# Feed-forward input products: the order of two loops in TensorE's stream

## The reference

```
def swiglu(h, w_in, w_out):
    gate, up = jnp.split(h @ w_in, 2, axis=-1)
    return (jax.nn.silu(gate) * up) @ w_out

x = x + 0.5 * swiglu(rmsnorm(x, norm_ffn1[layer]), w_ffn1_in[layer], w_ffn1_out[layer])
# mixer: retention in layer 0, sparse attention (indexer, top-k, latents) in layer 1
x = x + 0.5 * swiglu(rmsnorm(x, norm_ffn2[layer]), w_ffn2_in[layer], w_ffn2_out[layer])
```

## Time and profile before

| | |
|---|---|
| median of 3 runs | 1981.36 us (1980.68 to 1982.73) |
| profiled execution | 1981.29 us |
| its span, first to last instruction | 1979.5 us |
| mean granted TensorE clock in it | 0.997 |
| TensorE busy | 1952.8 us, 99% |
| VectorE busy | 1446.8 us, 73% |
| ScalarE busy | 887.1 us, 45% |
| low parts of group products (VectorE L1544) | 280, 1217 ns each |
| high parts of group products (ScalarE L1019) | 280, 1063 ns each |

### The profile page before, as it was taken

One profiled execution on the slowest core, in us unless ns is written; L12 is line 12 of the kernel. 1 busy time (PEld: TensorE's weight loads), 2 busy tenths in 40 slices (PEclk: granted clock), 3 DMA queues, 4 the chain that ended last, 5 costly groups with the idle time before them and its releaser, 6 DMA issues.

```text
span 1979.5 us, 23580 instructions
## 1 busy us (share of the span) xinstructions
PE 1952.8 (99%) x9152; PEld 1611.3 (81%) x9152; DVE 1446.8 (73%) x1838; ACT 887.1 (45%) x1240; POOL 219.3 (11%) x163
## 2 busy tenths in 40 slices
PE   8999999999999999999999999999999999999998
PEld 7788888878787878888888888888897888888886
DVE  7999953876666859999943899984358769989732
ACT  5545632342424435545621555562168445554510
POOL 0000011100000022000021000002145440000121
PEclk9999999999999999999999999999999999999999
DMA  4224132331313230332232333222222014222221
GB/s 171 86 101 154 45 116 75 144 133 43 134 43 133 84 130 1 118 138 86 73 103 75 112 140 115 86 88 98 88 87 84 1 43 170 86 85 100 102 98 62
DMA packets 76189, 189.53 MB, mean 96 GB/s; under 512 B 4144, under 2 KB 12336, under 8 KB 73008
## 3 DMA queue, kind: packets, MB, share of 16 engines
q1 hardware_dynamic: 76080, 188.04, 27.2%
HBM read 185.92 MB, written 2.10 MB: 95 GB/s over the span
## 4 chain that ended last, share of the span: by engine, by line
PE 88%; DVE 7%; issue 2%; ACT 2%; SPq 0%; DMA 0%; POOL 0%; DVEq 0%; ACTq 0%
PE bank L2399 12%; PE bank L2401 12%; PE bank L2400 12%; PE bank L2391 12%; PE bank L2393 12%; PE bank L2392 12%; PE bank L2620 3%; PE bank L2618 3%; PE bank L2619 3%; PE bank L2644 2%; PE bank L2499 2%; DVE part_lo L1544 1%; PE bank L2629 1%; PE bank L2874 1%; PE bank L2819 1%
## 5 line engine op out<-in xcount | busy, mean ns | idle before, releaser
L1019 ACT ACTIVATE part_hi<-quad_w 128x1024 fp32r<-128x1024 f32 x280 | 293.2, 1063 | 278.1 <-PE bank L2401 192.8
L1544 DVE TENSOR_TENSOR part_lo<-quad_w,part_hi 128x1024 fp32r<-128x1024 f32 x280 | 329.9, 1217 | 25.6 <-ACT part_hi L1019 25.3
L2391 PE MATMUL bank<-gated_hi,out_hi 128*128 128x512 f32 x704 | 274.8, 390 | 0.0
L2393 PE MATMUL bank<-gated_hi,out_lo 128*128 128x512 f32 x704 | 274.0, 389 | 0.0
L2392 PE MATMUL bank<-gated_lo,out_hi 128*128 128x512 f32 x704 | 273.9, 389 | 0.0
L2399 PE MATMUL bank<-part_hi,s_hi 128*128 128x512 f32 x640 | 253.1, 396 | 3.7 <-DVE part_lo L1544 3.7
L2401 PE MATMUL bank<-part_hi,s_lo 128*128 128x512 f32 x640 | 249.9, 391 | 0.0
L2400 PE MATMUL bank<-part_lo,s_hi 128*128 128x512 f32 x640 | 249.9, 390 | 0.0
L2399 PE MATMUL bank<-part_hi,xn_hi 128*128 128x512 f32 x608 | 237.5, 391 | 4.3 <-DVE part_lo L1544 4.2
L2401 PE MATMUL bank<-part_hi,xn_lo 128*128 128x512 f32 x608 | 236.7, 389 | 0.0
L2400 PE MATMUL bank<-part_lo,xn_hi 128*128 128x512 f32 x608 | 236.6, 389 | 0.0
(11 more groups left out here) (300 smaller groups left out, 3418.9 us busy)
## 6 DMA issues: line engine op xcount, KB each, us to landing
quad_w<-w_ffn_in SPq DMA_DIRECT2D x80, 1024.0 KB, 7.3
out_raw<-w_ffn_out SPq DMA_DIRECT2D x64, 704.0 KB, 4.1
quad_w<-w_ret_in SPq DMA_DIRECT2D x14, 1024.0 KB, 7.4
rest_raw<-w_ffn_in SPq DMA_DIRECT2D x32, 256.0 KB, 5.3
quad_w<-w_ret_in SPq DMA_DIRECT2D x16, 512.0 KB, 5.4
quad_w<-w_ret_out SPq DMA_DIRECT2D x8, 1024.0 KB, 5.6
w_raw<-w_dsa SPq DMA_DIRECT2D x7, 1024.0 KB, 4.8
x_res<-x_in SPq DMA_DIRECT2D x8, 256.0 KB, 6.4
```

The lines of the kernel that those rows point to most:

```text
L1019: nc.scalar.activation(in_four(part_hi[part_slot(h)]), source, copy).then_inc(part_hi_made, 1)
L1544: nc.vector.tensor_tensor(in_four(part_lo[part_slot(h)]), source, in_four(part_hi[part_slot(h)]).bitcast(FP32), ALU.subtract)\
L2391: mm(to, w_hi_of[:, at:at + width], hi, start=start, stop=False)
L2393: return mm(to, w_lo_of[:, at:at + width], hi, start=False, stop=stop)
```

## The change

The token block becomes the outer loop, and half and chunk the inner ones: TensorE goes through all four chunks for the first token block, in its bank, and then through all four again for the second. The waits for the parts and for the S3 sum are written in both passes. `part_used` is raised only in the second pass, after the part's last matmul there. The matmuls, their operands and their number stay the same, and so do all other engines' streams.

```
                     name = PRODUCTS[i]
                     to = {"x11w11": 0, "x12w21": 0, "S2T2": 2, "S3T3": 2, "x22T4": 2, "S1T1": 4, "S4w22": 4}[name]
-                    for half in range(2):
-                        h = part_of(g, i, half)
-                        pe.wait_ge(part_lo_made, parts0 + h + 1)
-                        for kk in range(2):
-                            k = 2 * half + kk
-                            if name == "S3T3" and g == 0:
-                                pe.wait_ge(s_lo_made, 7 * m + (2 if s == 0 else 3) + k + 1)
-                            for t in range(2):
+                    for t in range(2):
+                        for half in range(2):
+                            h = part_of(g, i, half)
+                            pe.wait_ge(part_lo_made, parts0 + h + 1)
+                            for kk in range(2):
+                                k = 2 * half + kk
+                                if name == "S3T3" and g == 0:
+                                    pe.wait_ge(s_lo_made, 7 * m + (2 if s == 0 else 3) + k + 1)
                                 hi, lo = left(name, k, t)
                                 done = product_of_parts(bank[to + t][:, :], hi, lo, part_slot(h), kk,
                                                         k == 0, k == HALF_CHUNKS - 1)
-                        done.then_inc(part_used, 1)
+                            if t == 1:
+                                done.then_inc(part_used, 1)
```

## The result

The changed kernel takes 1983.90 us (median of 20 runs, 1983.08 to 1984.63), the kernel before 1980.95 us in the same comparison (20 runs, 1980.51 to 1982.73): ratio 1.0015, 95% interval 1.0009 to 1.0021, 2.95 us slower. The profiled execution took 1983.31 us with a span of 1981.5 us.

A forecast was written before the change was run, and what follows sets the result against it. TensorE was taken as the bound in steady groups, so only new TensorE waits count: 0 + 1.3 + 1.3 + 0.35 = 2.95 us on 1981.29 us, 1984.24, stated as 1984.3 us; range for 8 in 10, 1981.4 to 1987.0 us.

The forecast's parts named there:

- Third and fourth sublayer, 1.3 us each: In product 0, matmul 7 waits 1.21 us for the second half's low part; with the restart, 1.3 us lost per sublayer.
- First sublayer, 0: In product 0, a new wait of 0.95 us and a restart, all taken back at later waits for VectorE: 0.
- the clock's drop at 41 us goes away and the kernel gets faster: Start-up: the 2.25 us idle is split, saving the 1.7 us clock drop; 1979.6 us if it helped, 2 in 100.
- Last sublayer, 0.35 us: Product 0 loses 1.3 us; 0.87 us and a 0.08 us restart come back at the 1655.59 us wait; 0.35 us stay.
- Products 1 to 6 of a first group, 0: Pairs are ready before their product, or the second comes 1.14 us after the first and is wanted at 1.36 us: 0.
- The slot (edit b), 0: First half's part slot is given back 1.36 us later; the delay ends in ScalarE's idle time with 0.3 us left: 0.
- Satisfied waits and twelve matmuls in one bank, 0: All products: 280 added waits, mostly already met, and twelve matmuls in a row into one bank were each taken as 0.
- The clock rival, 7 in 100: The clock drops after the new waits, 1.7 us in each of three sublayers: 5.1 us more, 1989.4 us; 7 in 100.
- The gain from it is 0: First result bank is complete 2.72 us sooner, but its readers wait for a count raised in the second token block: 0.
- A measurement of this kernel tells no less than 0.2%: Whole kernel: differences within 0.2%, 4.0 us, count as no change; 77 in 100 for landing within.

The follow-up runs named there:

- experiment 1: The changed kernel, but product 0 of each sublayer's first group keeps the old order (136 of 140 products have the new one): 1980.52 us, ratio 1.000.
- experiment 2: The kernel before, with the new order only in product 0 of each sublayer's first group (4 of 140 products): 1984.10 us, ratio 1.0017.
- 11: The change as it is, product 0 included, plus a semaphore telling readers when the first bank is complete: 1982.16 us, ratio 1.0005 to the kernel before.
- experiment 8: The kernel before, with one small Silu ahead of product 0's second high part in the last sublayer, to load its table early: 1980.24 us, ratio 0.9997.
- experiment 3: The kernel before, with only the first half's part slot given back later, after 21 of 24 matmuls instead of 12: 1980.81 us, ratio 1.000.
- experiment 4: The kernel before in its old order, but TensorE waits for both parts of each product before its first matmul: 1993.57 us, ratio 1.0061.
- experiment 7: The kernel of experiment 4 plus six extra matmuls ahead of product 0's wait in the third, fourth and last sublayer: 1988.46 us, ratio 1.0039 to the kernel before.
- experiment 10: New order except in first groups' product 0, plus first-bank semaphore, early Silu table and six extra matmuls in the mixer's stand: 1977.88 us, 0.9987 to the kernel before.

## Why the prediction was right

1984.3 us were predicted and 1983.9 us measured. The mechanism is the predicted one, and the experiments tie it down: product 0 alone makes the loss (1 and 2). That the forecast and the medians both say 2.95 us is partly luck: the interval goes from 1.8 to 4.2 us, and the stages of the profiles, without the mixer's clock, add up to 2.8 us.

- *Third and fourth sublayer, 1.3 us each:* 1.36 and 1.34 us. Shown by the timelines and experiments 1 and 2.
- *First sublayer, 0:* -0.13 us in the profile of the change; in experiment 2 the new stand is there and the one at 41 us shrinks by as much. The prediction also weighed, at 2 in 100, that the clock's drop at 41 us goes away and the kernel gets faster, and said that VectorE's chain would make this worth nothing. So it came: the drop is gone in the changed kernel and in experiments 2 and 11, and the time saved ends in the stand at 55 us, 2.3 to 2.4 us in place of 0.77 us. The 1979.6 us given for that case left out the other terms; with them it would have been 1982.6 us.
- *Last sublayer, 0.35 us:* 0.49 us. The term was too small by the restart: I took 0.08 us off for it, but the first product behind transposes starts as slowly without a wait (0.48 us for its first matmul, against 0.47 us after the stand), so only the 0.87 us came back. The reading behind the term was wrong in one point: the part waited for at 1655.59 us does not hang on VectorE alone. VectorE itself stands for 1.07 us at 1649.11 us for ScalarE, which loads a table for 1.28 us first; with the table loaded early the stand is gone (experiment 8). The 0.87 us held, as this chain starts with product 0 and not with its matmul 7.
- *Products 1 to 6 of a first group, 0:* wrong for S1T1 of the last sublayer. The prediction had the second part of a pair come 1.14 us behind the first; here ScalarE's table load comes between them, and with the new order S1T1 waits 0.54 us for it (experiment 1). In the changed kernel the stand in product 0 covers this, so the sum did not feel it.
- *The slot (edit b), 0:* right, and with more cover than reckoned. The prediction had the price begin once the high part was 0.3 us later than its margin; in experiment 3 that margin is gone, and nothing is lost.
- *Satisfied waits and twelve matmuls in one bank, 0:* experiment 1, within 1.8 us by the times; by the timelines the lateness moves by 0.01 us from the third sublayer's S1T1 to the fourth's product 0.
- *The clock rival, 7 in 100:* it did not come. The new stands leave the clock at 1.00; experiment 4 shows it behind three stands of 2.4 us, and experiment 7 that it costs 1.7 us each, which is the price that the rival was given.
- *"The gain from it is 0":* right for the change as made. The reason given, that no reader knows of the bank, is right too. But the words behind it, that TensorE never waits in steady groups, were wrong by 0.05 us a group and 0.34 us at a sublayer's end: I read the waits of matmuls and not those of weight loads. Had the change come with a semaphore, this reading would have put it 1.6 us too high.
- *"A measurement of this kernel tells no less than 0.2%":* with 20 runs on each side it told 0.15%.

## What to carry to other kernels

When a loop order changes, list for each operand when it is now asked for and when its buffer is given back, and compare both with the rows of the stage's first pass, where producers start late; here the steady passes had the slack and the first did not. Finishing a result early can pay only if a semaphore tells its reader, and then it may pay in either order. Look at weight-load waits beside matmul waits before calling TensorE free of stalls.

## What the runs showed of the hardware

Stands of TensorE of 1.05 us in the middle of full work left the granted clock at 1.00 each time (three each in the changed kernel and in experiments 2, 7 and 11). Stands of 2.40 and 2.41 us took it to its lower level, 1.2 GHz, three times out of three, for 1.7 us of loss each (5.1 us in three, experiments 4 and 7). One of 2.18 us did so in ten profiles out of twelve. Six extra matmuls that nobody reads, put into each of the three stands of 2.4 us, took the drops away. The length of a stand alone does not decide. Of six stands of 2.34 to 2.38 us at 55 to 57 us in the start-up, three left the clock at 1.00 (the changed kernel and experiments 7 and 11), and three took it down (experiments 2, 3 and 8). And near 9 us stands of 1.81 to 2.01 us took it down in three profiles (the changed kernel and experiments 7 and 8), where 2.04 us in the kernel before and 3.31 us in experiment 10 did not. The Trainium skill, "TensorE: Matmul & The Clock Gate", section "A second HAM failure mode: psum-queue depth-cycling", tells of short idle times between groups of matmuls that bring the clock down again and again; these runs agree for most of the longer stands named here, not for all, and not for the 1.05 us ones. The profile of one execution can hide a quarter of an effect: the mixer's clock drop, present or absent, moved it by 0.8 us where the change is worth 2.95 us.
